# Rate sums' transfers on GpSimd, weights' rests on VectorE outside the feed-forwards, bias tables copied in DRAM, state-space output transposed in other banks

## What is computed

```
acum_l = jnp.cumsum(a, axis=2)                                       # state-space rates
decay_in = exp(where(causal, acum[..., :, None] - acum[..., None, :], -inf))
cum = jnp.cumsum(log_sigmoid(f_logit), axis=1)                       # forgetting attention
s = q @ k * scale + (cq[..., :, None] - cum[..., None, :])
s_own = s_own + bias_ht[:, rel_bucket(dist_own)][None]               # moba
s = where(mask, s + bias, -inf)                                      # sliding window
y = rmsnorm(y * silu(z), norm_w)                                     # state-space output
h = h + swiglu(rmsnorm(h), w_gate, w_up, w_down)
```

## Time and profile before

| what | us |
|---|---|
| median of 3 runs | 1255.49 |
| lowest, highest run | 1253.69, 1258.89 |
| the profiled execution's own time | 1250.67 |
| its span, first to last instruction | 1249.4 |
| TensorE busy | 1194.6 |
| VectorE busy | 682.3 |
| ScalarE busy | 591.9 |
| GpSimd busy | 473.1 |

### The profile page before, as it was taken

The page is one execution under the profiler, slowest core; times in us unless marked ns, Lnnn a source line. Parts: engine busy times, 40 slices in busy tenths (PEclk is TensorE's granted clock), DMA queues, the critical chain, the costliest instruction groups (busy, mean ns, idle before and its releaser), DMA issues.

```text
span 1249.4 us, 19584 instructions
## 1 busy us (share of the span) xinstructions
PE 1194.6 (96%) x8237; PEld 1096.5 (88%) x8237; DVE 682.3 (55%) x965; ACT 591.9 (47%) x901; POOL 473.1 (38%) x253
## 2 busy tenths in 40 slices
PE   7979999999989999999899999999999769999998
PEld 6979898788878999988898879999889768999986
DVE  5742644366756645334789757433326696633423
ACT  6534544445444554444652345444334674544432
POOL 4345333233231444441654423444423350543440
PEclk9989999999989999999999999999999879999999
DMA  7585465344445666564543435755555333756560
GB/s 240 163 265 154 145 197 144 108 121 125 128 135 152 184 188 187 187 200 143 182 134 135 151 120 171 217 177 185 196 185 173 114 135 118 217 181 187 177 199 34
DMA packets 160833, 204.75 MB, mean 164 GB/s; under 512 B 13535, under 2 KB 135577, under 8 KB 160746
## 3 DMA queue, kind: packets, MB, share of 16 engines
q1 hardware_dynamic: 154650, 193.69, 49.9%
q0 software_dynamic: 1840, 6.64, 1.6%
q10 hardware_dynamic: 4256, 3.16, 0.8%
HBM read 202.38 MB, written 1.09 MB: 163 GB/s over the span
## 4 chain that ended last, share of the span: by engine, by line
PE 78%; DVE 12%; ACT 6%; issue 2%; SPq 1%; ACTq 1%; DMA 0%; POOL 0%; DVEq 0%
PE bank L488 15%; PE bank L491 15%; PE bank L494 15%; PE bank L505 9%; PE bank L511 9%; PE bank L508 9%; ACT whi L947 2%; DVE wlo L1360 2%; DVE sm L1649 1%; PE bank L846 1%; DVE Ss L1780 1%; DVE ring L1651 1%; DVE uc L1490 1%; DVE qT L1774 1%; DVE ring L1637 1%
## 5 line engine op out<-in xcount | busy, mean ns | idle before, releaser
L1920 POOL TENSOR_TENSOR wlo<-raw,whi 128x1024 fp32r<-128x1024 f32 (+1 forms) x161 | 411.6, 2559 | 545.4 <-ACT whi L947 545.4
L947 ACT ACTIVATE whi<-raw 128x1024 fp32r<-128x1024 f32 x368 | 364.9, 1041 | 125.7 <-PE bank L511 117.0
L1360 DVE TENSOR_TENSOR wlo<-raw,whi 128x1024 fp32r<-128x1024 f32 x207 | 277.9, 1352 | 258.9 <-ACT whi L947 257.9
L488 PE MATMUL bank<-hh,whi 128*128 128x256 f32 x1792 | 293.7, 286 | 1.7 <-ACT hh L979 1.7
L491 PE MATMUL bank<-hh,wlo 128*128 128x256 f32 x1792 | 289.4, 284 | 0.9 <-DVE wlo L1360 0.9
L494 PE MATMUL bank<-hl,whi 128*128 128x256 f32 x1792 | 289.0, 284 | 0.0
L488 PEld LDWEIGHTS bank<-hh,whi 128*128 128x128 f32 x1792 | 248.8, 193 | 11.1 <-issue 9.9
L491 PEld LDWEIGHTS bank<-hh,wlo 128*128 128x128 f32 x1792 | 248.3, 193 | 1.4 <-DVE wlo L1360 1.4
L494 PEld LDWEIGHTS bank<-hl,whi 128*128 128x128 f32 x1792 | 248.4, 193 | 0.0
L505 PE MATMUL bank<-whi,gh 128*128 128x512 f32 x264 | 83.4, 397 | 0.0
L511 PE MATMUL bank<-whi,gl 128*128 128x512 f32 x264 | 83.1, 395 | 0.0
(11 more groups left out here) (296 smaller groups left out, 1319.0 us busy)
## 6 DMA issues: line engine op xcount, KB each, us to landing
raw<-in_ffn_w_in SPq DMA_DIRECT2D x88, 512.0 KB, 3.6
raw<-in_w_in SPq DMA_DIRECT2D x72, 512.0 KB, 3.7
raw<-in_ffn_w_out SPq DMA_DIRECT2D x44, 512.0 KB, 3.2
raw<-in_hgrn_w_in SPq DMA_DIRECT2D x32, 512.0 KB, 4.0
raw<-in_w_ffn_gate SPq DMA_DIRECT2D x22, 512.0 KB, 4.6
raw<-in_w_ffn_up SPq DMA_DIRECT2D x22, 512.0 KB, 4.1
raw<-in_w_ffn_down SPq DMA_DIRECT2D x22, 512.0 KB, 3.3
raw<-in_w_branch SPq DMA_DIRECT2D x16, 512.0 KB, 4.1
```

Of the source, the lines that this page charges most:

```text
L488: T.matmul(out, wh[:, i, c], xh[:, k, :], start=first and (i, k) == pairs[0], stop=False)
L947: A.activation(half_of(whi, j, h), half_of(raw, j, h), ACT.Copy).then_inc(s_hi[j % NS][h], 1)
L1360: V.tensor_tensor(half_of(wlo, j, h), half_of(raw, j, h), half_of(whi, j, h).bitcast(f32), ALU.subtract).then_inc(s_lo[j % NS][h], 1)
L1920: G.tensor_tensor(half_of(wlo, j, 1), half_of(raw, j, 1), half_of(whi, j, 1).bitcast(f32), ALU.subtract).then_inc(s_lo[j % NS][1], 1)
```

## The change

- The store of the rate sums and the eight transfers that spread them go from ScalarE's queue to GpSimd's, behind the store of the bias rows. GpSimd's waits for weights between them go, since it has no rests there.
- `on_pool` gives GpSimd the second halves of units 2 to 30 of each feed-forward and no others; all others are VectorE's.
- GpSimd, between the masks of the decay rows and those of the forgetting rows, copies the 16 bias rows in DRAM into 128 copies each (`u_copies`, 16 x 128 x 384). The tables are then loaded from the copies, each partition one element less far, so that they arrive in order. The flips, their fills, ScalarE's copies and the constant `flip` go; the fills of the first attention are spread over its ten steps without them. VectorE waits for the tables at the second attention's first logits.
- The transposed state-space output goes to banks 3 and 7.

```
-        starts = [unit_at[k] for k in (("g", 0, 0), ("hf", 0), ("g", 1, 0), ("lu", 0), ("g", 2, 0))] + [NU]
+        light = [(unit_at["g", f, 0] + 2, unit_at["g", f, 0] + 31) for f in range(3)]
 
         def on_pool(j, h):
-            return h == 1 and (j < 2 or j > 2) and all(not u - 2 <= j < u + 2 for u in starts)
+            return h == 1 and any(u0 <= j < u1 for u0, u1 in light)
...
-        FOX = [[("gate", 1, 0)], [("gate", 1, 1), ("ym",)], [("gate", 1, 2)], [("gate", 1, 3)], [("b", 0), ("b", 1)], [("b", 2)],
-               [("b", 3), ("bv",)], [("br", 0, 0)], [("br", 0, 1), ("win", 0)], [("win", 1), ("win", 2)]]
-        FOX_REST = [("win", c) for c in range(3, 8)]
+        FOX = [[("gate", 1, 0)], [("gate", 1, 1), ("ym",)], [("gate", 1, 2)], [("gate", 1, 3)], [("b", 0)], [("b", 1)],
+               [("b", 2), ("b", 3)], [("bv",)], [("br", 0, 0)], [("br", 0, 1)]]
...
-                        b = turn(("ym", c), 4 + c)
+                        b = turn(("ym", c), (3, 7)[c])
...
-                    T.matmul(banks[b][:, :], flip[:, :], windows_of(c), start=True, stop=True).then_inc(s_full[b], 1)
...
-                    aq.wait_ge(*evac("sums"))
-                    A.dma_start(a["sums_scratch"], sums[:, :]).then_inc(s_sums, 16)
-            aq.wait_ge(s_sums, 16)
-
-            for rows, h0, parts in ((dec_rows, 0, ((0, 0, 256), (256, 128, 128))), (fox_rows, 8, ((0, 0, 128), (128, 0, 256)))):
-                for c0, s0, n in parts:
-                    for i, heads in enumerate((5, 3)):
-                        src = bass.AP(a["sums_scratch"].tensor, (h0 + 5 * i) * 256 + s0, [[0, 128], [256, heads], [1, n]])
-                        A.dma_start(rows[i][:, :, c0:c0 + n], src).then_inc(s_spread[h0 // 8], 16)
...
-                    A.activation(windows_of(what[1]), bank_of(*what)[:, :], ACT.Copy).then_inc(evacuated(*what), 1)
...
                     if n == 1:
                         vq.wait_ge(s_masked, 2)
+                    else:
+                        vq.wait_ge(s_w, 32)
...
             G.dma_start(a["u_scratch"], rb[0:16, 16:400]).then_inc(s_u, 16)
-            use(("cv", 1), 0)
+            gq.wait_ge(*evac("sums"))
+            G.dma_start(a["sums_scratch"], sums[:, :]).then_inc(s_sums, 16)
+            gq.wait_ge(s_sums, 16)
+
+            for rows, h0, parts in ((dec_rows, 0, ((0, 0, 256), (256, 128, 128))), (fox_rows, 8, ((0, 0, 128), (128, 0, 256)))):
+                for c0, s0, n in parts:
+                    for i, heads in enumerate((5, 3)):
+                        src = bass.AP(a["sums_scratch"].tensor, (h0 + 5 * i) * 256 + s0, [[0, 128], [256, heads], [1, n]])
+                        G.dma_start(rows[i][:, :, c0:c0 + n], src).then_inc(s_spread[h0 // 8], 16)
...
                 if i == 0:
-                    use(("gate", 0, 1))
+                    gq.wait_ge(s_u, 16)
+                    G.dma_start(a["u_copies"], a["u_scratch"].rearrange("h (o n) -> h o n", o=1).broadcast_to([16, 128, 384])).then_inc(s_copies, 16)
...
-                    gq.wait_ge(s_u, 16)
+                    gq.wait_ge(s_copies, 16)
...
-                        src = bass.AP(a["u_scratch"].tensor, 8 * i * 384, [[1, 128], [384, 8], [1, 256]])
+                        src = bass.AP(a["u_copies"].tensor, 8 * i * 128 * 384 + 127, [[383, 128], [128 * 384, 8], [1, 256]])
                         G.dma_start(dst, src).then_inc(s_w, 16)
...
+    args["u_copies"] = nc.dram_tensor("u_copies", (16, 128, 384), f32, kind="Internal").ap()
```

More of the change, by code:

```diff
@@ L754, in fill, with attention @@
                         tok.then_inc(s_full[b], 1)
[L755 to L760, removed]
-                    T.matmul(banks[b][:, :], flip[:, :], windows_of(c), start=True, stop=True).then_inc(s_full[b], 1)
-            def attention(n, fills, rest, inputs):
+            def attention(n, fills, inputs):
                 q, k, v, heads_k, window, slot = ATT[n]
@@ L803, in attention @@
                         values(i - 2)
[L804 to L810, removed]
+            attention(1, FOX, [("col", "c", j) for j in range(4)] + [("tok", "cv", t) for t in range(2)])
+            attention(2, MOBA, [("col", "b", j) for j in range(4)] + [("tok", "bv", t) for t in range(2)])
+            attention(3, SWA, [("col", "d", 0), ("col", "d", 1), ("col", "dk"), ("dv",)])
             branch(3, 0)
@@ L1124, in fill, with attention @@
                         A.activation(bh[:, 0, 2 * c:2 * c + 2, :], two(bank_of("ym", c)[:, :]), ACT.Copy).then_inc(s_bt, 1)
-                else:
-                    aq.wait_ge(*full(*what))
-                    A.activation(windows_of(what[1]), bank_of(*what)[:, :], ACT.Copy).then_inc(evacuated(*what), 1)
-            def attention(n, fills, rest):
+            def attention(n, fills):
                 slot = ATT[n][5]
@@ L1171, in attention @@
                         values_out(i - 2)
-                for what in rest:
-                    fill(what)
-            attention(1, FOX, FOX_REST)
-            attention(2, MOBA, [])
-            attention(3, SWA, [])
+            attention(1, FOX)
+            attention(2, MOBA)
+            attention(3, SWA)
             branch(3, 0)
@@ L1620, in fill, with attention @@
                                         ALU.subtract).then_inc(evacuated("ym", c), 1)
-                elif what[0] != "win":
+                else:
                     use(what)
-            def attention(n, fills, rest):
+            def attention(n, fills):
                 window, slot = ATT[n][4:]
@@ L1943, in gpsimd_program @@
             G.memset(vec[0:1, :], 1.0).then_inc(s_const, 1)
-            diagonal(flip, -127, 1).then_inc(s_const, 1)
             G.memset(half[:, :], -0.5).then_inc(s_const, 1)
@@ L1987, in fill @@
                     for i, dst in enumerate((wmoba, wswa)):
-                        src = bass.AP(a["u_scratch"].tensor, 8 * i * 384, [[1, 128], [384, 8], [1, 256]])
+                        src = bass.AP(a["u_copies"].tensor, 8 * i * 128 * 384 + 127, [[383, 128], [128 * 384, 8], [1, 256]])
                         G.dma_start(dst, src).then_inc(s_w, 16)
-                elif what[0] != "win":
+                else:
                     use(what)
-            for fills in (*FOX, FOX_REST, *MOBA, *SWA):
+            for fills in (*FOX, *MOBA, *SWA):
                 for what in fills:
```

8 lines of the change are left out of this document (3 added, 5 removed).

## The result

The changed kernel takes **1223.2 us** (median of four runs, 1222.4 to 1226.9) against 1254.6 of the kernel before beside it: ratio 0.975, 95% interval 0.972 to 0.979. A later set of runs gave 1224.5 against 1250.5, ratio 0.979 (0.977 to 0.981). The profiled execution took 1223.8 us with a span of 1222.5, 26.9 us less than the span of before.

A forecast was written before the change was run, and what follows sets the result against it. TensorE, busy 96% of the span, was taken as the bound. Terms of 8.7, 6.0, 8.2, 0.9, 0.5 and 1.0 sum to 25.3 us off 1250.67, 1225.4; with 4.8 us to the median, 1230 us, range 1217 to 1246.

The forecast's parts named there:

- Spreads, 8.7 us: First mixer, about 90 us: TensorE's 6.50 us wait for ScalarE goes, plus 2.25 of the low clock behind it.
- the forecast's late end of 98.4: First mixer: GpSimd's masks of the decay rows end at 93.1 to 98.4; ScalarE wants them at 96.
- Banks, 6.0: Third forgetting head's scores: the 3.02 us wait for VectorE and low clock behind it go; bounds 3.0 and 7.0.
- Flips, 8.2: First and second attention: 16 flips at 0.455 us each and a 0.92 us wait for ScalarE's copy go.
- Copy, 0: First mixer: the 3.15 MB copy of bias rows stays hidden, some 15 to 30 us long; bounds 0 and 4.
- End of the third attention, 0.9: TensorE's 2.98 us wait for `ring`: the line ahead becomes 2.19 us shorter, 1.22 is added, 0.9 gained.
- more than forecast: Rival, 0.11: VectorE halves TensorE's HGRN and LRU idle time and the 2.98 us go whole; about 1221 us.
- End of the second attention, 0.5; LRU, 1.0; HGRN, 0: Gains from moved rests: 0.5 us estimated; LRU stage 1, bounds -3 and 4; HGRN 0, bounds -8 and +3.
- The step from execution to median, 4.8 us: The runs' median lay 4.8 us above the profiled execution; keeping that distance turned 1225.4 into 1230 us.
- The slower rival: HGRN, LRU stage and attention tails: every moved rest costs VectorE its full price, 35.6 against 22.9 us gained; 1268 us, 0.06.
- that of the new wait: First mixer: late transfers or copy make ScalarE wait at the decay exponents, taking part back; 1236 to 1242 us, 0.16.
- That the change would do nothing: Rival, 0.05: other waits stand behind those removed, only the flips' columns are gained and lost elsewhere; within 6 us of before.

The follow-up runs named there:

- the swapped spreads: Changed kernel with the forgetting rows' four spreads issued ahead of the decay rows' four: 1224.3 us, ratio 0.979; the changed kernel gave 1224.5.
- the four copies: Changed kernel with the bias rows copied four times instead of once, table loads behind all four: 1235.5 us, ratio 0.987, 11 us slower than the changed kernel.
- The two rests moved alone: Kernel before with only the last two of GpSimd's rests of the third attention given to VectorE: 1246.5 us against 1250.5, ratio 0.996.
- eight took all of it: Kernel before with only all eight of GpSimd's rests from the third attention's own units given to VectorE: 1247.1 us against 1250.5, ratio 0.998.

## Why the prediction was right, and where it was not

1230 us were forecast, 1217 to 1246, and 1223.2 came. Its own sum for the profiled execution, 1225.4, stands against 1223.8. That is closer than its terms are, and in part luck: 4.5 us more than forecast came at the end of the third attention, and 3.8 us that no term foresaw were lost at the start.

- **Spreads, 8.7 us:** 9.4 in the trace, 9.7 alone. ScalarE's issuing was the wait. The masks ended at 98.8, just past the forecast's late end of 98.4, because GpSimd's store went out at 80.3, not 76.5 (TensorE was 3.8 us later from the start on). ScalarE wanted them at 99.9, not 96, in part for the same reason, so nothing showed. The decay rows' spreads landed after 6.3 to 8.0 us, between the two rows taken as bounds; on ScalarE's queue, in the kernel before, they landed after 5.7 to 7.0, and with the spreads alone on GpSimd's after 4.8 to 6.6. The forgetting rows, issued behind them, landed later: after 7.2 to 10.4 us, against 6.4 to 6.8 on ScalarE's queue; with the order swapped it was the decay rows that took 8.3 to 9.7. So the four issued last land later on GpSimd's queue, for a cause that no run shows. The Trainium skill, "SBUF — State Buffer", section "SBUF: two separate sides", in its box, warns that transfers issued from GpSimd can starve beside VectorE in a two-port operation. These runs hardly test it: while GpSimd issued the four decay spreads, from 83.68 to 87.04 us, VectorE stood until 86.69.
- **Banks, 6.0:** 6.1 and 6.5. **Flips, 8.2:** 8.2 and 8.7. **Copy, 0:** it took 18.4 us, within the 15 to 30 estimated; the reason given (the weights beside the window loads did not wait) was too weak, as the four copies show.
- **End of the third attention, 0.9: the step that failed.** The prediction replaced 2.19 us by 1.22 in the last head alone. VectorE saves such an amount in every head whose rest moves, and since TensorE runs ahead of it there, the savings add up until the last head. The two rests moved alone show it (1.0 us a head). The 2.98 us went whole, and with them 2.6 us of low clock: from the start of these transposes, TensorE reaches the thirteenth group of two of the last branch's products after 8.46 us before (361.68 to 370.14) and after 5.89 now (338.52 to 344.41). The rival *more than forecast* had this wait going whole; its other half, TensorE's idle time in HGRN and the LRU stage, was not halved: 5.7 became 6.0 us and 18.8 became 17.1.
- **End of the second attention, 0.5; LRU, 1.0; HGRN, 0:** 0.5, 1.3 and 0; with the rests alone 0.5, 1.5 and 0. For the LRU stage that is little more than the 1.1 us by which kernels without an edit there differ. HGRN is the clearest case of return: 16 rests more on VectorE, and its busy time there falls from 127.4 of 161 to 120.4 of 160 us.
- **Not foreseen:** 3.8 us lost in the first 54 us of the profiled execution. The prediction counted what GpSimd no longer does and not what it then issues sooner (two row loads at 11.6 instead of 16 us); that can bear on the 2.2 us lost by 24 us, and it stays open whether it does. The other 1.6 us are the low clock at 47 us, which kernels without the change show too.
- **The step from execution to median, 4.8 us:** the three runs shown were a high sample. In the later sets the kernel before has medians of 1250.4 to 1251.4, about the profiled execution's own 1250.67. This was most of the distance between 1230 and 1223.

The slower rival (VectorE becomes the bound) is refuted by the rests alone, which gained; that of the new wait by the masks' place in time and the swapped spreads. That the change would do nothing is refuted by each part alone.

## What to carry to other kernels

Where one engine runs ahead of another through a loop, a saving in each turn can be invisible until the loop ends, and there it appears added up over the turns, until the follower has caught up (two rests took 2.07 us off a wait of 2.98, eight took all of it and no more): look at how far the follower lies behind at each turn, not at the last wait alone. A wait is worth itself and the low clock behind it, and the low clock can go when the wait only gets shorter. A loss in one profiled execution is not yet the change's: look at the same stretch in kernels that leave it alone. A transfer called free should be tried several times over: that shows how wide its cover was.

## What the runs showed of the hardware that was not expected

- GpSimd and VectorE hold each other up in both directions. The four masks take 4.38 us with two of VectorE's rests beside them (2.91 us for the two, where 2.36 is usual), and 2.40 in the kernel with the spreads swapped, where no rest ran beside them. The Trainium skill, "SBUF — State Buffer", section "SBUF: two separate sides", tells of an exclusive lock held for a whole instruction; both directions agree with it. VectorE's two rests beside the masks in the changed kernel, then the masks with the spreads swapped:

```profile
95.06 2.91 DVE L1332 TENSOR_TENSOR wlo<-raw,whi 128x1024 fp32r<-128x1024 f32 x2 [3.48 <-ACT whi L933]
```

```profile
96.21 2.40 POOL L1946 TENSOR_SCALAR_AFFINE_SELECT decs<-decs 128x640 f32<-128x640 f32 x4 [9.11 <-DMA decs<-sums_scratch]
```

- Even an operation on two columns pays the whole price: VectorE's sum of 128x2 took 2.34 us (median) beside a rest on GpSimd and takes 0.15 without.
- A wait of 2.98 us at the end of the third attention had a granted clock of 0.57 behind it; one of 0.91 us at the same place had 1.00.
